# Making both parts of each weight chunk on GpSimd in a two-layer streaming encoder step

## The reference

```python
z = _rmsnorm(x, g_mix[0]) @ w_in_even[0]             # layer 0: 2600 columns
x = x + concatenate([y_a, y_b]) @ w_out_even[0]
z = _rmsnorm(x, g_mix[1]) @ w_in_odd[0]              # layer 1: gate and recurrent branch
r = sigmoid(xr @ w_a + b_a); ig = sigmoid(xr @ w_i + b_i)
a = exp(-8 * r * softplus(-lam)); b = sqrt(1 - a * a) * ig * xr
h = scan(a, b)                                       # h[t] = a[t] * h[t-1] + b[t]
x = x + (gelu(gate) * h) @ w_out_odd[0]
# every layer l
k, v = hm @ w_xk[l], hm @ w_xv[l]                    # hm: normalised memory, 256 tokens
x = x + attention(h @ w_xq[l], k, v) @ w_xo[l]
val, g = split(_rmsnorm(x, g_ffn[l]) @ w_up[l])
x = x + (gelu(causal_conv(g)) * val) @ w_down[l]
```

## Time and profile before

| | |
|---|---|
| median of 3 runs | 1795.16 us (1789.87 to 1797.14) |
| profiled execution, span on the core | 1793.0 us |
| PE busy | 1686.0 us (94%) |
| DVE busy | 1011.7 us (56%) |
| ACT busy | 637.6 us (36%) |
| POOL busy | 598.9 us (33%) |
| DMA, mean over the span | 86 GB/s |

### The profile page before, as it was taken

The page is one execution under the profiler, slowest core; times in us unless marked ns, Lnnn a source line. Parts: engine busy times, 40 slices in busy tenths (PEclk is TensorE's granted clock), DMA queues, the critical chain, the costliest instruction groups (busy, mean ns, idle before and its releaser), DMA issues.

```text
span 1793.0 us, 30718 instructions
## 1 busy us (share of the span) xinstructions
PE 1686.0 (94%) x11894; PEld 1568.9 (88%) x11894; DVE 1011.7 (56%) x1355; ACT 637.6 (36%) x913; POOL 598.9 (33%) x239
## 2 busy tenths in 40 slices
PE   6999879999899999999999879799999999999999
PEld 5959853599689999999999778689869999999999
DVE  5769985356635554056655766755645655136640
ACT  4332234343523332133333356533434333123321
POOL 2314320043123343343343244543203334334332
PEclk9969997899999999999999989999999999999999
DMA  4322330024012223222232222232402222222232
GB/s 164 122 79 95 99 127 1 1 82 174 27 48 82 82 82 102 74 82 82 97 103 75 73 70 95 87 109 83 153 9 85 81 83 95 86 77 82 82 109 83
DMA packets 41711, 153.46 MB, mean 86 GB/s; under 512 B 5344, under 2 KB 5856, under 8 KB 40360
## 3 DMA queue, kind: packets, MB, share of 16 engines
q1 hardware_dynamic: 41640, 152.46, 25.4%
HBM read 145.22 MB, written 9.32 MB: 86 GB/s over the span
## 4 chain that ended last, share of the span: by engine, by line
issue 52%; PE 27%; POOL 11%; DVE 7%; ACT 1%; DMA 0%; POOLq 0%; SPq 0%; DVEq 0%; ACTq 0%
PE PS L745 25%; POOL WLO L380 11%; DVE SC L1193 1%; DVE M L1192 1%; PE AX L842 1%; DVE YC L1243 1%; DVE SQA L1105 0%; DVE YC L1248 0%; ACT RL L528 0%; DVE WLO L1257 0%; POOLq L406 0%; DVE CB L1228 0%; DVE CB L1093 0%; PE AX L797 0%; DMA WRAW<-in_w_mv 0%
## 5 line engine op out<-in xcount | busy, mean ns | idle before, releaser
L380 POOL TENSOR_TENSOR WLO<-WRAW,WHI 128x1024 fp32r<-128x1024 f32 (+1 forms) x231 | 598.4, 2592 | 1150.0 <-ACT WHI L420 1149.9
L745 PE MATMUL PS<-XH,WHI 128*128 128x274 f32 x2256 | 479.6, 294 | 35.4 <-POOL WLO L380 26.1
L420 ACT ACTIVATE WHI<-WRAW 128x1024 fp32r<-128x1024 f32 (+1 forms) x237 | 262.5, 1107 | 695.9 <-PE PS L745 657.5
L745 PE MATMUL PS<-XH,WLO 128*128 128x274 f32 x2256 | 476.1, 292 | 0.0
L745 PE MATMUL PS<-XL,WHI 128*128 128x274 f32 x2256 | 473.5, 291 | 0.0
L745 PEld LDWEIGHTS PS<-XH,WHI 128*128 128x128 f32 x2256 | 362.3, 191 | 41.4 <-issue 19.0
L745 PEld LDWEIGHTS PS<-XL,WHI 128*128 128x128 f32 x2256 | 361.1, 191 | 0.0
L745 PEld LDWEIGHTS PS<-XH,WLO 128*128 128x128 f32 x2256 | 360.7, 191 | 0.0
L745 PE MATMUL PS<-HH,WHI 128*128 128x274 f32 x1216 | 256.8, 292 | 1.8 <-POOL WLO L380 1.1
L745 PE MATMUL PS<-HH,WLO 128*128 128x274 f32 x1216 | 254.3, 290 | 0.0
L745 PE MATMUL PS<-HL,WHI 128*128 128x274 f32 x1216 | 254.2, 291 | 0.0
(11 more groups left out here) (231 smaller groups left out, 1735.1 us busy)
## 6 DMA issues: line engine op xcount, KB each, us to landing
WRAW<-in_w_in_even SPq DMA_DIRECT2D x29, 512.0 KB, 3.5
WRAW<-in_w_up0a SPq DMA_DIRECT2D x22, 512.0 KB, 3.4
WRAW<-in_w_up0b SPq DMA_DIRECT2D x22, 512.0 KB, 3.5
WRAW<-in_w_up1a SPq DMA_DIRECT2D x22, 512.0 KB, 3.4
WRAW<-in_w_up1b SPq DMA_DIRECT2D x22, 512.0 KB, 3.4
WRAW<-in_w_mv SPq DMA_DIRECT2D x16, 512.0 KB, 3.5
WRAW<-in_w_xq SPq DMA_DIRECT2D x16, 512.0 KB, 3.5
WRAW<-in_w_xo SPq DMA_DIRECT2D x16, 512.0 KB, 3.5
```

What stands on the lines that cost most here:

```text
L380: pool.tensor_tensor(WLO[parity][:, 0:cols], WRAW[parity][:, 0:cols], WHIf[parity][:, 0:cols], ALU.subtract).then_inc(lo_done, 1)
L420: act.activation(WHI[parity][:, 0:cols], WRAW[parity][:, 0:cols], ACT.Copy).then_inc(hi_done, 1)
L745: ins = pe.matmul(dst, w, x, start=first, stop=last)
```

## The change

ACT's function `hi` and all of its calls (`ahead` too) are removed. POOL gets a `hi` of its own, a `tensor_copy` with the same waits as before, which stands directly ahead of the `lo` of the same chunk. POOL's hardware loops are replaced by 237 turns written out. For chunks 31 to 36 POOL makes the high part and DVE the low part, as before. The two memsets behind these chunks come after POOL's `hi(36)`. Nothing else is changed: the computation, the loads, the buffers, PE's and DVE's programs are the same.

```diff
         @block.gpsimd
         def _(pool):
-            def lo(c, cols, parity):
-
+            def hi(c):
+
+                cols = slice(0, COLS[c])
+                pool.wait_ge(raw_landed[c % 2], 16 * (c // 2) + 16)
+                if c >= 2:
+                    pool.wait_ge(chunk_done, c - 1)
+                pool.tensor_copy(WHI[c % 2][:, cols], WRAW[c % 2][:, cols]).then_inc(hi_done, 1)
+
+            def lo(c):
+
+                cols = slice(0, COLS[c])
                 pool.wait_ge(hi_done, c + 1)
-                pool.tensor_tensor(WLO[parity][:, 0:cols], WRAW[parity][:, 0:cols], WHIf[parity][:, 0:cols],
+                pool.tensor_tensor(WLO[c % 2][:, cols], WRAW[c % 2][:, cols], WHIf[c % 2][:, cols],
                                    ALU.subtract).then_inc(lo_done, 1)
...
-            c = 0
-            while c < N_CHUNKS:
...
-                with pool.Fori(0, n) as i:
-                    for k in range(2):
-                        lo(i * 2 + (c + k), pair[k], (c + k) % 2)
-                c += 2 * n
+            for c in range(N_CHUNKS):
+                hi(c)
+                if c not in DVE_LO:
+                    lo(c)
+                if c == DVE_LO.stop - 1:
+                    pool.wait_ge(lo_done, DVE_LO.stop)
                     pool.wait_ge(chunk_done, C0["out_even"])
                     unused_columns(A_TILES, KT)
...
         @block.scalar
         def _(act):
-            def hi(c, parity, cols, turn):
-
-                act.wait_ge(raw_landed[parity], turn * 16 + 16)
-                if not isinstance(c, int) or c >= 2:
-                    act.wait_ge(chunk_done, c - 1)
-                act.activation(WHI[parity][:, 0:cols], WRAW[parity][:, 0:cols], ACT.Copy).then_inc(hi_done, 1)
...
                 with act.Fori(0, HALF_T - 2) as i:
-                    hi(i * 2 + (c0 + 4), c0 % 2, 1024, i + (c0 + 4) // 2)
-                    tile(i + 1, lambda: hi(i * 2 + (c0 + 5), (c0 + 1) % 2, 1024, i + (c0 + 5) // 2))
-                ahead(c0 + 20)
-                tile(HALF_T - 1, lambda: ahead(c0 + 21))
+                    tile(i + 1)
+                tile(HALF_T - 1)
```

More of the change, by code:

```diff
@@ L388, in _ @@
             unused_columns(0, A_TILES)
-            c = 0
-            while c < N_CHUNKS:
-                if c == DVE_LO.start:
-                    c = DVE_LO.stop
-                    pool.wait_ge(lo_done, c)
+            for c in range(N_CHUNKS):
[4 more added lines that the diff above has]
+                    pool.wait_ge(lo_done, DVE_LO.stop)
                     pool.wait_ge(chunk_done, C0["out_even"])
                     unused_columns(A_TILES, KT)
[L398 to L405, removed]
-                with pool.Fori(0, n) as i:
-                    for k in range(2):
-                        lo(i * 2 + (c + k), pair[k], (c + k) % 2)
-                c += 2 * n
-            assert c == N_CHUNKS
         @block.scalar
         def _(act):
-            def hi(c, parity, cols, turn):
-                act.wait_ge(raw_landed[parity], turn * 16 + 16)
-                if not isinstance(c, int) or c >= 2:
-                    act.wait_ge(chunk_done, c - 1)
-                act.activation(WHI[parity][:, 0:cols], WRAW[parity][:, 0:cols], ACT.Copy).then_inc(hi_done, 1)
-            def ahead(c):
-                if c + 2 < N_CHUNKS:
-                    hi(c + 2, c % 2, COLS[c + 2], (c + 2) // 2)
             def norm_tile(norm, m, k):
@@ L594, in cross @@
                 c0, u0, t0 = C0[f"xq{l}"], HN0[f"xq{l}"], T0[f"xq{l}"]
-                ahead(c0)
                 std(READS[f"xq{l}"])
@@ L643, in ffn_up, with tile @@
                 q0 = FF_T * l + f0
-                def tile(f, between):
+                def tile(f):
                     act.wait_ge(gb_ready, f + (q0 + 1))
@@ L650, in tile @@
                     act.activation(GE[:], YB[:], ACT.Gelu_apprx_tanh).then_inc(gelu_done, 1)
-                    between()
                     act.wait_ge(evicted, f * 2 + (t0 + 2))
                     act.activation(HH[:, f, :], H32[:], ACT.Copy).then_inc(hh_ready, 1)
-                ahead(c0)
                 if half == "a":
                     std(READS[ph])
-                tile(0, lambda: ahead(c0 + 1))
+                tile(0)
                 with act.Fori(0, HALF_T - 2) as i:
-                    hi(i * 2 + (c0 + 4), c0 % 2, 1024, i + (c0 + 4) // 2)
-                    tile(i + 1, lambda: hi(i * 2 + (c0 + 5), (c0 + 1) % 2, 1024, i + (c0 + 5) // 2))
-                ahead(c0 + 20)
-                tile(HALF_T - 1, lambda: ahead(c0 + 21))
+                    tile(i + 1)
+                tile(HALF_T - 1)
             def softplus():
@@ L674, in _ @@
                     for m in range(KT):
-                        ahead(c0 + m)
                         if m == 0:
@@ L697, in _ @@
                                        bias=HB[:, 8 + m:9 + m]).then_inc(gates_read, 1)
-                        if m == 0:
-                            ahead(c0)
                         act.wait_ge(r_ready, m + 1)
                         act.activation(RU[:], RIG[:, 0, :], ACT.Tanh, scale=SP[:, m:m + 1]).then_inc(ta_done, 1)
-                        if m:
-                            ahead(c0 + 2 * m)
                         if m >= 2:
@@ L712, in _ @@
                             act.activation(RM2[:], RM2[:], ACT.Sqrt).then_inc(mult_ready, 1)
-                        ahead(c0 + 2 * m + 1)
                         if m % 2:
@@ L718, in _ @@
                     for m in range(8):
-                        ahead(C0["mv1"] + m)
                         if m == 0:
```

20 lines of the change are left out of this document (removed).

## The result

| | before | after |
|---|---|---|
| median | 1794.87 us (1789.87 to 1797.14, 4 runs) | 1818.3 us (1817.44 to 1819.84, 4 runs) |
| span of the profiled execution | 1793.0 us | 1815.7 us |
| after / before | | 1.0137, 95% interval 1.0121 to 1.0153 |

A forecast was written before the change was run, and what follows sets the result against it. The prediction took TensorE, busy 1686.0 of 1793.0 us, as the bound, with DVE pacing some stages; 3 + 18 + 8 + 13 - 5 + 0 = +37 us gave 1830 us (1786 to 1880).

The forecast's parts named there:

- the port: SBUF port pair shared by POOL and DVE: DVE's copies, scans and two-input instructions would wait for whole POOL casts.
- The cast: POOL's price per high part: 1.2 us at 1024 columns, 1.5 at 1280, 1.6 at 1408.
- recurrent input: Recurrent input projection, 8 chunks: between 0 and 9.6 us possible, the walk gave +3.
- the FFN up loop: FFN up, 88 chunks: a pair just fits its 12.28 us, so 0; tips at a cast of 1.4 us.
- the tail with memory values: Convolution tail and memory values of layer 0, 28 casts: between 0 and 33.6 us possible, the walk gave +13.
- The starts: Six stage starts after a normalisation, where ACT's copy precedes the square root: 1 us gained at five, -5.
- the gate stage: Four turns of two tiles, 28.5 us each: casts put a POOL instruction ahead of each scan, +4.5 a turn, +18.
- memory values of layer 1: Eight chunks in 39 us: POOL needs 3.7 us a chunk with DVE's work between, +8, lasting 47 us.
- The down projections: FFN down stages: 8.4 us a chunk for 1.6 + 3.2 us of POOL work, so 0.
- The second: Rival, waits for POOL's low part (39.3 us) go: 1768 if DVE takes back half; faster by over 0.5%, chance 0.13.
- The third: Rival: the two effects cancel, or the cast doesn't take the lock, 1794 us; chance 0.12.
- The first: Rival: cast of 1.4 us or longer tips the FFN loop, costing 19 to 32 us there, 1860 to 1885; chance 0.2.

The follow-up runs named there:

- the last run: Kernel before, but POOL casts chunks 0 and 1, ACT's norm-start square roots precede copies, and copies precede tanh in gate tiles three, five, seven: 1779.7 us.
- the extra copy: Kernel before with POOL's loop written out, POOL also copying 231 raw chunks into the low part's buffer ahead of the subtract: 1824.6 us.
- the long cast: Changed kernel with each cast replaced by a two-operand POOL addition of the raw chunk to itself: 1871.2 us.
- the run with ACT's waits: Changed kernel, but ACT keeps the waits of its former high parts at their old places, without the copies: 1825.3 us.

## Why the prediction was right, and where it was wrong

**Right: the port, and the cast in it.** DVE's instructions lengthen beside casts as the prediction said, and the change is slower for it. The cast costs less than I took: 1.04 us undisturbed and 1.104 in the mean at 1024 columns, 1.36 at 1408, against my 1.2 and 1.6. That is the lower end, ACT's copy. From the two lengths, (1.36 - 1.04)/384 gives 0.83 ns a column and 0.19 us fixed. By the Trainium skill (GPSIMD Engine Reference, Engine selection) one-input work is roughly at line rate, from which the prediction's estimate was 0.85 us with a fixed part on top; 1024 columns at 0.83 ns agree with it.

**Right in size: recurrent input** (+3 forecast, +4.6). PE's waits for POOL there, 9.8 us, went, and DVE's eviction of RCV took 15.7. The port's cost changed its place: the three tiny copies, which had waited for a subtract, fell from 15.6 to 6.3 us over the stage, and the taps, HL and ML behind them rose from 31.0 to 48.3.

**Right by luck: the FFN up loop** (0 forecast, 0). In the walk the second tap ran ahead of the next cast, and the loop was to tip when it no longer did. The changed kernel, POOL, then DVE:

```profile
653.36 1.04 POOL L383 CAST WHI<-WRAW 128x1024 fp32r<-128x1024 f32 x1 [2.25 <-PE PS L696]
654.49 2.77 POOL L389 TENSOR_TENSOR WLO<-WRAW,WHI 128x1024 fp32r<-128x1024 f32 x1
```
```profile
653.47 1.52 DVE L1345 SCALAR_TENSOR_TENSOR YB<-GB,PR,YB 128x548 f32<-128x548 f32 x1
655.72 2.12 DVE L1348 TENSOR_TENSOR GE<-GE,RSTD 128x548 f32<-128x548 f32 x1 [0.73 <-ACT GE L612]
```

The cast comes first and the tap waits for it, then the next instruction waits for the subtract, and the pair still lasts 12.28 us. The step "with a cast of 1.4 us the second tap starts behind the cast ... and the loop no longer fits" is wrong: it starts behind a cast of 1.04, and the loop fits.

**Right in the sum only: layer 0.** I gave +13 to the tail with memory values. They took 6.5; another 5.7 went into the input projections ahead of them, to which I had given nothing (2.4 of it is a new PE wait for DVE's low part XL; the rest was not taken apart). By luck these two make 12.2.

**The starts** were forecast at -5. The change shows -1.9 at the first product, -1.4 at each FFN start: -4.7, and +0.6 to +0.8 at the query projections, with the scatter at both that the last run showed.

**Wrong: the gate stage, +18 forecast, +1.0 measured.** The step that failed is "with eight POOL instructions a turn instead of four, each of the four scans finds one ahead of it. The walk gives +4.5 a turn". The blocking itself is there. The changed kernel in one turn, POOL, then DVE:

```profile
1105.44 3.34 POOL L389 TENSOR_TENSOR WLO<-WRAW,WHI 128x1024 fp32r<-128x1024 f32 x1
1109.09 1.82 POOL L383 CAST WHI<-WRAW 128x1280 fp32r<-128x1280 f32 x1 [0.31 <-PE PS L696]
1110.99 3.87 POOL L389 TENSOR_TENSOR WLO<-WRAW,WHI 128x1280 fp32r<-128x1280 f32 x1
1115.37 1.04 POOL L383 CAST WHI<-WRAW 128x1024 fp32r<-128x1024 f32 x1 [0.51 <-PE PS L696]
1116.49 2.34 POOL L389 TENSOR_TENSOR WLO<-WRAW,WHI 128x1024 fp32r<-128x1024 f32 x1
```
```profile
1106.54 3.32 DVE L1422 TENSOR_TENSOR_SCAN RB<-RA,RB 128x512 f32<-128x512 f32 x1
1109.79 1.21 DVE L1422 TENSOR_TENSOR_SCAN RB<-RA,PR,RB 128x32 f32<-128x32 f32 x1
1110.91 1.19 DVE L1422 TENSOR_TENSOR_SCAN RB<-RA,RB 128x512 f32<-128x512 f32 x1
1112.03 2.91 DVE L1422 TENSOR_TENSOR_SCAN RB<-RA,PR,RB 128x32 f32<-128x32 f32 x1
...
1116.91 2.60 DVE L1158 SCALAR_TENSOR_TENSOR MK<-MK,PR,SQA 128x256 f32<-128x256 f32 x2
...
1120.94 0.42 DVE L1152 TENSOR_TENSOR MK<-PS,RM 128x256 f32<-128x256 f32 x1
```

The two 32-column scans lose 1.0 and 2.7 us (0.25 when alone) and the normalisation 1.7 (0.88 alone), 5.3 us in all against the 4.5 a turn that I forecast. (It is not each of the four scans, as I had it: the long ones take what they took before. DVE's busy time in the stage rose by 22 us, 5.5 a turn.) But before, PE stood there for 4.5 us anyway, for a low part that was late behind ACT's tanh. Now the low part is early, PE does the gates' products of the chunk at once, and stands for 4.8 us ahead of the key product, for DVE's eviction L1152. One wait took the place of another, of the same length. The forecast added DVE's delay to a turn that already held POOL's delay. The second and third turn of two tiles took 29.3 and 28.4 us (from the third tile's first product at 1074.97 to the fifth's at 1104.26 and the seventh's at 1132.66) where they had taken 28.2 and 27.7, not the 32 to 33 that I had named. The last run bears this out from the other side: with the low part early in three of the tiles and no cast on POOL the gates last 8.7 us less.

**Wrong: memory values of layer 1, +8 forecast, 0 measured.** The same error, with POOL at both ends. PE waited 8.7 us for POOL there before, when POOL itself stood for ACT's high parts, and waits 8.8 now, in six short waits instead of three. POOL now works almost without a pause from 1175 on, at 4.3 us a chunk (cast 1.5, subtract 2.7, both lengthened by DVE) where I had 3.7. With the extra copy, which keeps ACT's order, the stage grows by 3.2 us; with the long cast by 12.0. That the two waits are of the same length is what this trace shows, and nothing says that it must be so.

**Wrong: "The down projections ... stay at 0".** That was a sum over a chunk's period and true inside the stage. It overlooked the boundary, where the 1408-column pair runs beside the last tile of an FFN: 2 x 3.8 us, a third of the whole cost.

**The rivals.** The second, faster, had DVE take back half of the 39.3 us; 29.3 of them did go, but DVE took 32.3. The third had the two effects cancel; in the gates and memory values of layer 1 they do, and only there. The first, the FFN loop tipping at a cast of 1.4 us, is refuted: it holds with 1.89 us in one piece. The sum was 14.4 us too high (37 against 22.6): 17, 8 and 6.5 too much in the gates, the memory values of layer 1 and the tail, against 7.6 in the down projections and 5.7 in the input projections that it had at nothing, 1.6 in the recurrent input, and 2.2 less gain in the rows of the starts (-2.8 to the first product, in the attention and in the two FFN halves, for the -5).

## What to carry to other kernels

Before adding a delay to a stage, look at what its slow engine waits for now: a wait that the change removes is slack for the one it brings, and the two replace each other instead of adding up. Walk the boundaries of stages as well as their periods, since a large tile's work starts beside the last small one. And when moving work to another engine to escape an engine's order, try the order first: here the same copies, all but two left on ACT and issued a few instructions earlier or later, give 15 us where moving them costs 23.

## What was not expected of the hardware

- A POOL memset, which reads nothing, makes DVE's three-column copies within SBUF last up to 1.2 us instead of 0.15, to its own end, while scans and two-operand instructions beside it keep their length.
- A two-operand POOL addition whose operands are the same tile took 1.89 us at 1024 columns; the subtract of two tiles takes 2.40.
- Between two POOL instructions 0.08 us apart three DVE copies of two columns got through (the run with the long cast).
- The attention stage of layer 0, with the same work, lasted 83.8 to 94.5 us, in step with its granted clock (0.85 to 0.74). Why the clock differs between executions, and whether the run with ACT's waits has more than chance in it, stays open.
